# Adding the causal mask of the stick-breaking heads on VectorE instead of by identity products on TensorE

## The reference, cut to what matters

```python
def stick_breaking_attention(q, k, v):
    ...
        z = jnp.einsum('bhqd,bhkd->bhqk', q[:, :, start:end], k[:, :, :end]).astype(jnp.float32) * scale
        mask = jnp.arange(end)[None, :] < jnp.arange(start, end)[:, None]
        log_beta = jax.nn.log_sigmoid(z)
        log_keep = jnp.where(mask, jax.nn.log_sigmoid(-z), 0.0)
        later = lax.cumsum(log_keep, axis=3, reverse=True) - log_keep
        w = jnp.where(mask, jnp.exp(log_beta + later), 0.0)
        outs.append(jnp.einsum('bhqk,bhkd->bhqd', w.astype(v.dtype), v[:, :, :end]))
```

## Time and profile before

| | us |
|---|---|
| median of 3 runs | 814.82 (813.75 to 815.11) |
| the profiled execution | 814.42 |
| its span in the profile | 812.2 |
| TensorE busy | 798.2 |
| VectorE busy | 647.5 |
| ScalarE busy | 483.8 |

### The profile page before, as it was taken

The page is one execution under the profiler, slowest core; times in us unless marked ns, Lnnn a source line. Parts: engine busy times, 40 slices in busy tenths (PEclk is TensorE's granted clock), DMA queues, the critical chain, the costliest instruction groups (busy, mean ns, idle before and its releaser), DMA issues.

```text
span 812.2 us, 16860 instructions
## 1 busy us (share of the span) xinstructions
PE 798.2 (98%) x6810; PEld 777.2 (96%) x6810; DVE 647.5 (80%) x1385; ACT 483.8 (60%) x1008; POOL 21.1 (3%) x53
## 2 busy tenths in 40 slices
PE   8999999999999999999999999899999999999998
PEld 7999998999999999999999999889889999999998
DVE  5889887988899886999988887977667896775551
ACT  6755566776666566745554646665655775555440
POOL 1000000000000000000000000700000000000000
PEclk9999999999999999999999999999999999999999
DMA  9777683666656987499998887545334578655540
GB/s 292 261 240 241 219 286 113 206 203 208 206 191 199 324 299 261 157 322 325 360 327 297 298 259 223 163 135 175 124 109 152 167 261 271 209 184 196 194 157 27
DMA packets 150014, 179.44 MB, mean 221 GB/s; under 512 B 5681, under 2 KB 139569, under 8 KB 149937
## 3 DMA queue, kind: packets, MB, share of 16 engines
q1 hardware_dynamic: 147680, 177.22, 65.5%
q10 hardware_dynamic: 1232, 1.11, 0.4%
q0 software_dynamic: 1024, 0.03, 0.1%
HBM read 177.27 MB, written 1.05 MB: 220 GB/s over the span
## 4 chain that ended last, share of the span: by engine, by line
PE 77%; DVE 4%; ACT 3%; issue 1%; DVEq 0%; ACTq 0%
PE bank L1396 24%; PE bank L1399 23%; PE bank L1400 23%; DVE wlo L979 1%; PE bank L1385 1%; PE bank L1503 1%; PE bank L1387 1%; PE bank L1386 1%; PE bank L1487 1%; PE bank L1520 0%; PE bank L1417 0%; PE bank L1449 0%; ACT whi L736 0%; PE bank L1466 0%; DVE yb L1019 0%
## 5 line engine op out<-in xcount | busy, mean ns | idle before, releaser
L979 DVE TENSOR_TENSOR wlo<-raw,whi 128x512 fp32r<-128x512 f32 x528 | 342.9, 684 | 66.9 <-ACT whi L736 66.4
L736 ACT ACTIVATE whi<-raw 128x512 fp32r<-128x512 f32 x528 | 306.9, 622 | 96.6 <-PE bank L1400 85.4
L1396 PE MATMUL bank<-A,whi 128*128 128x256 f32 x1152 | 323.6, 281 | 2.8 <-DVE wlo L979 2.0
L1399 PE MATMUL bank<-A,whi 128*128 128x256 f32 x1152 | 319.5, 277 | 0.1
L1400 PE MATMUL bank<-A,wlo 128*128 128x256 f32 x1152 | 319.1, 277 | 0.0
L1396 PEld LDWEIGHTS bank<-A,whi 128*128 128x128 f32 x1152 | 217.3, 189 | 4.4 <-DVE wlo L979 2.2
L1399 PEld LDWEIGHTS bank<-A,whi 128*128 128x128 f32 x1152 | 217.2, 189 | 0.8 <-issue 0.5
L1400 PEld LDWEIGHTS bank<-A,wlo 128*128 128x128 f32 x1152 | 217.0, 188 | 0.0
L1396 PE MATMUL bank<-Hhi,whi 128*128 128x256 f32 x528 | 146.0, 276 | 0.0
L1400 PE MATMUL bank<-Hhi,wlo 128*128 128x256 f32 x528 | 145.7, 276 | 0.0
L1399 PE MATMUL bank<-Hlo,whi 128*128 128x256 f32 x528 | 145.7, 276 | 0.0
(11 more groups left out here) (160 smaller groups left out, 956.7 us busy)
## 6 DMA issues: line engine op xcount, KB each, us to landing
mring<-in_w_mod SPq DMA_DIRECT2D x72, 512.0 KB, 6.4
raw<-in_ffn_w_up SPq DMA_DIRECT2D x22, 1024.0 KB, 5.1
raw<-in_w_gate SPq DMA_DIRECT2D x22, 1024.0 KB, 5.6
raw<-in_w_up SPq DMA_DIRECT2D x22, 1024.0 KB, 5.8
raw<-in_w_down SPq DMA_DIRECT2D x16, 1024.0 KB, 5.8
raw<-in_w_in SPq DMA_DIRECT2D x12, 1024.0 KB, 5.8
raw<-in_moba_w_qkv SPq DMA_DIRECT2D x11, 1024.0 KB, 6.4
raw<-in_ffn_w_down SPq DMA_DIRECT2D x8, 1024.0 KB, 7.1
```

The lines of the kernel that those rows point to most:

```text
L736: act.activation(whi[:, i % SPL, k0:k1, 0:width], raw[:, i % RAW, k0:k1, 0:width], ACT.Copy).then_inc(s_whi, 1)
L979: dve.tensor_tensor(lo, raw[:, i % RAW, k0:k1, 0:width], hi.bitcast(F32), ALU.subtract).then_inc(s_wlo, 1)
L1396: pe.matmul(o, hi, xh, start=kg == 0 and not (j and halved(g)), stop=False)
L1399: pe.matmul(o, hi, xl, start=False, stop=False)
```

## The change

TensorE no longer adds the mask: the eight products at L1444 go, and `s_scores` is raised by the last score product of each head. VectorE gets a function `hide`, called in the step `scores`: it waits for `s_scores` and adds `negs` to columns 0 to 255 of the head's bank, in place (128x256, in the kernel after at L1286). It raises a new semaphore, `s_masked`. ScalarE's Abs (L912) waits for `s_masked` instead of `s_scores`.

```diff
@@ build_program, ScalarE, first_pass
-                    need.wait_ge(s_scores, n + 1)
+                    need.wait_ge(s_masked, k)
@@ VectorE
             def peaks(n):
-                if heads[n][0] != "sb":
-                    peak(n)
-                    peak(n + 1)
+                for m in (n, n + 1):
+                    if heads[m][0] != "sb":
+                        peak(m)
+                    else:
+                        hide(m)
+
+            def hide(n):
+                z = head_bank(n)[:, 0:S].rearrange("p (a b) -> p a b", a=2)
+                need.wait_ge(s_scores, n + 1)
+                need.wait_ge(s_const, n_const)
+                dve.tensor_tensor(z, z, negs[:, :].unsqueeze(1).broadcast_to([P, 2, P]), ALU.add).then_inc(s_masked, 1)
@@ TensorE, scores
                 if kind == "sb":
                     for o0, o1, k0, q0 in ((P, 3 * P, 0, 0), (0, P, P, P)):
                         for b, q, k in pair:
-                            pe.matmul(b[:, o0:o1], k[:, k0:k0 + P], q[:, q0:S], start=q0 == 0, stop=False)
-                    for b, q, k in pair:
-                        ins = pe.matmul(b[:, 0:S], identb[:, :], negs[:, :].unsqueeze(1).broadcast_to([P, 2, P]), start=False, stop=True)
-                        ins.then_inc(s_scores, 1)
+                            ins = pe.matmul(b[:, o0:o1], k[:, k0:k0 + P], q[:, q0:S], start=q0 == 0, stop=q0 > 0)
+                            if q0 > 0:
+                                ins.then_inc(s_scores, 1)
                     return
```

More of the change, by code:

```diff
@@ L519, in build_program @@
         s_tpe, s_tfree, s_w, s_val, s_ohi, s_olo = (sem(n) for n in ("s_tpe", "s_tfree", "s_w", "s_val", "s_ohi", "s_olo"))
-        s_lsum, s_vn, s_rcol = sem("s_lsum"), sem("s_vn"), sem("s_rcol")
+        s_masked, s_lsum, s_vn, s_rcol = sem("s_masked"), sem("s_lsum"), sem("s_vn"), sem("s_rcol")
         s_gq, s_qsq, s_qln, s_qr, s_qkn = (sem(n) for n in ("s_gq", "s_qsq", "s_qln", "s_qr", "s_qkn"))
```

## The result

| | before | after |
|---|---|---|
| median, both kernels measured side by side on one chip, us | 814.29 (813.60 to 815.11) | 818.73 (818.34 to 818.89) |
| the profiled execution | 814.42 | 818.34 |
| its span | 812.2 | 816.0 |

The kernel became slower: the ratio after to before is 1.0051, with a 95% interval of 1.0035 to 1.0067, 4.4 us of the medians. The prediction was 819.0 us in a range of 817.2 to 820.8.

A forecast was written before the change was run, and what follows sets the result against it. TensorE was taken as the bound, busy 798.2 of 812.2 us. Delays of 3.42 us (pairs one and two) and 1.15 us (three and four) sum to 4.57, on 814.42 giving 819.0 us, range 817.2 to 820.8.

The forecast's parts named there:

- one addition: VectorE, each of eight 128x256 mask additions: taken as 0.42 us, from the subtraction that reads a bank.
- first L912 late: First pair: additions stand behind two `wlo` passes, so ScalarE's L912 starts at 523.61, 2.59 us later.
- first wait of `later`: First pair, TensorE at L1487: waits 2.26 us for `stick_sum`, where it had reached it without a wait.
- second pair, L912 late: Second pair: additions stand where a `wlo` pass was, so ScalarE's L912 moves from 529.08 to 532.64, 3.56 us.
- TensorE late after two pairs: TensorE's last L1487 of pairs one and two moves from 537.88 to 541.30, 3.42 us late.
- third pair, added: Third pair: L912 moves from 567.90 to 568.14, and TensorE waits 0.24 us more for L1306.
- third and fourth pair: Fourth pair's L912 starts 1.15 us later, third pair's 0.24 included, with no slack behind: 1.15 us for both pairs.
- The products' saving eaten by waits: TensorE: removed products save 0.12 us per pair of them, 0.5 for four, not credited because TensorE waits right behind.
- TensorE's list of waits: Sign in the profile after: L1487 waits on VectorE 5 to 6 us, in pieces of about 2.3, 1.1, 0.8, 1.6.
- The clock rival: TensorE's clock falls to half behind the new waits, 1.7 us of lost work: 819.5 to 820.7 us; chance 25%.
- Second pair free: Slack behind 529.08 hides the second pair's delay, leaving 2.26, 0.24 and part of the fourth pair's: 816.9 us; 10%.
- Not slower: Longer path to L1487 stays inside the first pair's 0.38 us slack, so TensorE's regained work decides: 813.9 us; 4%.

The follow-up runs named there:

- the run with both: Changed kernel with the eight products kept as well, so the mask is added twice; 819.31 against 814.11 us for the kernel before, ratio 1.0068.
- the run of half the change: Additions at pairs one and two only, products kept at three and four; 817.38 against 813.99 us for the kernel before, ratio 1.0042.
- the run of the other half: Additions at pairs three and four only, products kept at one and two; 815.18 us, ratio 1.0017 to the kernel before.
- the work alone: Kernel before, products kept, plus eight same-size VectorE additions on a scratch tile nobody waits for; 814.49 against 813.99 us, ratio 1.0005.
- the run with the additions one step later: Changed kernel with the first pair's additions moved behind the modulation pass in VectorE's queue; 820.87 us, ratio 1.0083 to the kernel before.
- the two new orders: Kernel before (products) and changed kernel (additions), VectorE's list reordered: 814.76, 814.60 us; second order, also moving six ScalarE steps: 811.14, 811.92 us.
- the additions earlier: Changed kernel with the first pair's additions moved ahead of two `wlo` passes in VectorE's queue; 817.66 against 814.22 us for the kernel before, ratio 1.0043.
- no mask: Kernel before with the stick-breaking heads' mask left out, neither products nor additions, so another output; 814.55 against 813.99 us, ratio 1.0001.

## Why the prediction was right

**The sum.** Predicted and measured, step by step:

| step of the prediction | predicted, us | measured, us |
|---|---|---|
| one addition | 0.42 | 0.42 |
| first L912 late | 2.59 | 522.89 + 0.73 - 521.02 = 2.60 |
| first wait of `later` | 2.26 | delay 2.29; as a wait 0.44 after, 2.12 in the run with both, where the clock held |
| second pair, L912 late | 3.56 | 3.57 |
| TensorE late after two pairs | 3.42 | 3.39 in the trace; 3.39 by the run of half the change |
| third pair, added | 0.24 | 0.32 |
| third and fourth pair | 1.15 | 1.25 in the trace; 1.19 by the run of the other half |
| all | 4.57 | 4.44 of the medians |

**The products' saving eaten by waits.** Shown by the traces: adding the products back to the changed kernel moved TensorE at no pair but the third, by 0.3 us, and there through the additions that wait for them. Leaving them out without a replacement changed the times by nothing that can be measured, and one trace by 0.27 us. The 0.12 us for a pair against the 0.22, the estimate from the Trainium skill (TensorE: Matmul & The Clock Gate, section Back-to-back issue gap), is not decided by either.

**TensorE's list of waits.** Predicted 5 to 6 us for L1487 (now L1494), in pieces of 2.3, 1.1, 0.8 and 1.6; measured 3.8, in pieces of 0.44, 0.83, 1.02 and 1.53. The delay was right and the form of it was not: the step that failed is "around the 1.6 us wait that began at 520.5 it stayed 1.00", from which I took that the clock would hold there. The wait was 1.94 us this time, longer because the two products that had ended 0.3 us closer to the eviction were gone. The clock fell behind it, and 1.7 us of the first wait turned into slow products. Its length does not explain the fall: with the work alone the clock fell behind 1.61 us.

**The clock rival.** I had put its place behind the first new wait, at 2.26 us, with 819.5 to 820.7 us as the outcome. In the profiled execution it came one wait earlier and was hidden. That it cost nothing was luck, since the sum had no term for it: of the four executions the one at clock 1.00 took 818.64 us and the three at 0.998 took 818.34 to 818.89, but with the work alone the same fall cost 1.6 us. The run with the additions one step later shows the rival as it was meant: a wait of 3.27 us, clock 0.50 behind it, by the medians 1.1 us more than the sum of delays. The Trainium skill (TensorE: Matmul & The Clock Gate, section Why this matters for your kernels) warns of longer gaps only; the trace disagrees, with 0.57 behind 1.94 us.

**Second pair free.** Excluded by the run with half of the change: 3.39 us, where this rival gives 2.3.

**Not slower.** Excluded at this place. Where VectorE takes the additions early, in the two new orders, the change cost 1 us or less (814.60 against 814.76 us by the medians of the first, about 1 us at full clock; 0.8 us in the second). At full clock it never made the kernel faster than the products in the same order.

## What to carry to other kernels

An instruction's price depends on its place in an in-order queue and on who waits for it: additions of 0.42 us behind two passes made TensorE 2.3 us late once another engine had to wait for them, and all eight with nobody waiting cost some 0.5 us, where the change cost 4.4. Follow such a delay engine by engine to the one that sets the time, and subtract the slack there. A better order on one engine alone moved the wait to the next one here; with ScalarE's steps moved too it gained 3.0 us, and then VectorE's queue was full and plain work seemed to count again.

## What was not expected of the hardware

- TensorE's clock fell from 2.4 GHz behind waits shorter than I had thought, and their length does not decide it. Behind the eviction's wait it fell to 0.5 to 0.66 after 1.94 us (the kernel after), 1.84 us (pairs one and two alone, and the additions earlier) and 1.61 us (the work alone). It stayed at 1.00 after another 1.84 us (the additions later, and no mask), 1.61 us (products and additions), 1.60 us (before) and 1.52 us (pairs three and four alone). At other waits it fell after 1.88 us (first new order, products) and stayed after 2.05 us (the same order, additions) and 2.12 us (products and additions, first pair). Before, a wait of 1.97 us at the program's start went with 0.50; the stretch 8.6 to 12.0 us read 1.00 in the kernel after and in every experiment. What decides is open. It differs between executions of one kernel too: with the products in the first new order five of eleven kept the clock and six did not.
- What such a fall costs depends on what comes next: 1.6 us with the work alone, where nothing hid it; nothing after, where the new wait took it up; and some 0.6 us at the first pair with the additions earlier, which the second pair's wait took up.
- The start of the program differs between executions as well: the same product, the first one behind ScalarE's squares, stands at 125.28 to 126.05 us in the fourteen traces. So two spans can differ by 0.8 us for a reason that has nothing to do with the change.
